# Attention heads taken two at a time on TensorE: scores by row halves into two banks, values by column halves

## The reference, cut to what matters

```python
scores = q[j] @ k[j].T / 8 + bias      # 256 x 256, only the causal three 128x128 blocks
p = softmax(scores)                    # diff heads: p = softmax(s0) - lam * softmax(s1)
out = p @ v[j]                         # 28 products: 8 moba, 4 diff (128 wide), 8 + 8 windowed
```

## Time and profile before

| what | value |
|---|---|
| median of 3 runs | 1296.03 us (1295.26 to 1300.27) |
| the profiled execution's own time | 1300.93 us |
| its span, first to last instruction | 1299.1 us |
| time outside the span | 1.8 us |
| mean granted TensorE clock | 0.988 of full speed |

### The profile page before, as it was taken

How to read it: one execution, slowest core, us unless ns; L and a number is a source line. 1 busy time by engine, 2 the same in 40 slices (tenths; PEclk the granted TensorE clock), 3 DMA queues, 4 the chain that set the end, 5 groups by cost and what they waited for, 6 DMA issues and landing times. The chain is left out here.

```text
span 1299.1 us, 27195 instructions
## 1 busy us (share of the span) xinstructions
PE 1257.0 (97%) x10208; PEld 1217.9 (94%) x10208; DVE 875.5 (67%) x1457; ACT 708.3 (55%) x1221; POOL 403.9 (31%) x376
## 2 busy tenths in 40 slices
PE   8998879799999999999999999999999999999997
PEld 7988779799999999998999999999988999999997
DVE  6656667577777765666667777855766567777755
ACT  4654558445566654555544666644455445666642
POOL 2020100722333421130135643413620237434313
PEclk9999989999999999999999999999999999999999
DMA  7633344466465666554565466666444563666662
GB/s 249 191 114 114 98 130 130 130 194 184 157 190 185 189 184 188 156 160 131 149 191 165 132 193 184 186 188 187 131 146 130 167 191 115 181 192 192 181 185 89
DMA packets 60288, 212.70 MB, mean 164 GB/s; under 512 B 6688, under 2 KB 7968, under 8 KB 60064
## 3 DMA queue, kind: packets, MB, share of 16 engines
q1 hardware_dynamic: 60192, 211.39, 53.4%
HBM read 210.31 MB, written 1.05 MB: 163 GB/s over the span
## 5 line engine op out<-in xcount | busy, mean ns | idle before, releaser
L1337 DVE TENSOR_TENSOR wlo<-raw,whi 128x1024 fp32r<-128x1024 f32 (+1 forms) x400 | 494.8, 1238 | 267.0 <-ACT whi L697 262.6
L1022 PE MATMUL bank<-xhi,whi 128*128 128x256 f32 x2240 | 642.0, 287 | 13.7 <-DVE wlo L1337 12.0
L1023 PE MATMUL bank<-xlo,whi 128*128 128x256 f32 x2240 | 628.5, 281 | 0.0
L1024 PE MATMUL bank<-xhi,wlo 128*128 128x256 f32 x2240 | 628.4, 281 | 0.0
L697 ACT ACTIVATE whi<-raw 128x1024 fp32r<-128x1024 f32 (+1 forms) x400 | 415.5, 1040 | 155.9 <-PE bank L1024 150.8
L1022 PEld LDWEIGHTS bank<-xhi,whi 128*128 128x128 f32 x2240 | 427.0, 191 | 30.6 <-DVE wlo L1337 17.0
L1024 PEld LDWEIGHTS bank<-xhi,wlo 128*128 128x128 f32 x2240 | 424.7, 190 | 0.0
L1023 PEld LDWEIGHTS bank<-xlo,whi 128*128 128x128 f32 x2240 | 423.0, 189 | 0.6
L598 POOL TENSOR_TENSOR fprod<-ugate,uval 128x256 f32<-128x256 f32 x66 | 92.0, 1394 | 213.3 <-DVE uval L1683 207.7
L1022 PE MATMUL bank<-fhi,whi 128*128 128x256 f32 x528 | 148.7, 282 | 0.0
L1024 PE MATMUL bank<-fhi,wlo 128*128 128x256 f32 x528 | 148.4, 281 | 0.0
(11 more groups left out here) (202 smaller groups left out, 1311.6 us busy)
## 6 DMA issues: line engine op xcount, KB each, us to landing
raw<-in_w_win SPq DMA_DIRECT2D x140, 512.0 KB, 3.5
raw<-in_w_up SPq DMA_DIRECT2D x132, 512.0 KB, 3.6
raw<-in_w_down SPq DMA_DIRECT2D x48, 448.0 KB, 3.5
raw<-in_w_merge SPq DMA_DIRECT2D x32, 512.0 KB, 4.0
raw<-in_w_out SPq DMA_DIRECT2D x24, 512.0 KB, 3.5
raw<-in_w_down SPq DMA_DIRECT2D x24, 512.0 KB, 3.5
x<-in_x SPq DMA_DIRECT2D x4, 256.0 KB, 4.9
rgw<-in_rg_w SPq DMA_DIRECT2D x1, 1024.0 KB, 10.6
```

The source lines that it names most:

```text
L1022: pe.matmul(ps, whi[:, slot, w], hi, start=first, stop=False)
L1023: pe.matmul(ps, whi[:, slot, w], lo, start=False, stop=False)
L1024: return pe.matmul(ps, wlo[:, slot, w], hi, start=False, stop=last)
L1337: dve.tensor_tensor(wlo[:, n % RING, w], raw[:, n % RING, w], whi[:, n % RING, w].bitcast(f32), ALU.subtract) \
```

## The change

Scores, values and their waits are regrouped by pairs of heads.

- TensorE "scores" takes two heads: their q and k lie in rows 0 to 63 and 64 to 127. The four matmuls go head A, head B (first 128 queries), head A, head B (the other 128). Head A writes `ps_score`, head B writes `ps_stat`, a bank that was free in these stages.
- TensorE "values" takes two 64-wide heads: A, B (first half of the keys), A, B (second half), head A to columns 0 to 63 and head B to columns 64 to 127 of one bank. Differential heads stay single.
- VectorE, ScalarE and GpSimd do in one "scores" step what they did in two, and read the bank of the head. "weights" stays one head at a time.
- The slots: moba scores in 13, 15, 17, 19, weights in 15 to 22 as before, values in 17, 19, 21, 23. Differential: turns of v one slot earlier (24, 25), scores in 25, 28, 31, 33, weights in 28, 31, 34, 36, values in 29, 32, 35, 37. Second and third layer: scores in 9, 13, 17, 21, weights in 11, 12, 15, 16, 19, 20, 23, 24, values in 13, 17, 21, 25.
- The order within a slot is now values, weights, scores; it was weights, scores, values.

```diff
-    for j in range(MOBA_H):
-        at(b + 13 + j, "scores", j)
-        at(b + 15 + j, "weights", j)
-        at(b + 16 + j, "values", j)
+    for pair in range(MOBA_H // 2):
+        at(b + 13 + 2 * pair, "scores", pair)
+        for i in range(2):
+            at(b + 15 + 2 * pair + i, "weights", 2 * pair + i)
+        at(b + 17 + 2 * pair, "values", 2 * pair)
     for half in range(NQT):
-        at(b + 25 + half, "turn_v", 1, half)
-    for j in range(2 * DIFF_H):
-        at(b + 26 + j, "scores", MOBA_H + j)
-        if j % 2:
-            at(b + 28 + j, "weights", MOBA_H + j // 2)
-            at(b + 29 + j, "values", MOBA_H + j // 2)
+        at(b + 24 + half, "turn_v", 1, half)
+    for h, n in enumerate((25, 28, 31, 33)):
+        at(b + n, "scores", MOBA_H // 2 + h)
+        at(b + n + 3, "weights", MOBA_H + h)
+        at(b + n + 4, "values", MOBA_H + h)
...
-        for j in range(8):
-            g = 16 + 8 * l + j
-            at(b + 9 + 2 * j, "scores", g)
-            at(b + 11 + 2 * j, "weights", MOBA_H + DIFF_H + 8 * l + j)
-            at(b + 12 + 2 * j, "values", MOBA_H + DIFF_H + 8 * l + j)
+        for pair in range(4):
+            w = MOBA_H + DIFF_H + 8 * l + 2 * pair
+            at(b + 9 + 4 * pair, "scores", MOBA_H // 2 + DIFF_H + 4 * l + pair)
+            for i in range(2):
+                at(b + 11 + 4 * pair + i, "weights", w + i)
+            at(b + 13 + 4 * pair, "values", w)
...
-    order = ("rg_split", "rg_scan", "turn_v", "turn_v2", "rope", "weights", "scores", "values")
+    order = ("rg_split", "rg_scan", "turn_v", "turn_v2", "rope", "values", "weights", "scores")
...
+        def score_bank(j):
+
+            return (ps_score, ps_stat)[j % 2]
...
-            def step_scores(j):
-                u, q, k, qp, kp, slope = head(j)
-                if j < 16:
-                    pe.wait_ge(copied, 12 if j < 8 else 24)
+            def step_scores(pair):
+                heads = (2 * pair, 2 * pair + 1)
...
-                wait(pe, logits, j)
-                pe.matmul(ps_score[:, 0:P], u[qp:qp + HD, q, 0:P], u[kp:kp + HD, k, 0:P], start=True, stop=True)
-                pe.matmul(ps_score[:, P:3 * P], u[qp:qp + HD, q, P:2 * P], u[kp:kp + HD, k, :], start=True, stop=True,
-                          skip_group_check=True).then_inc(scored, 1)
+                wait(pe, logits, 2 * pair)
+                for rows, cols, across in ((0, P, P), (P, S, S)):
+                    for j in heads:
+                        u, q, k, qp, kp, slope = head(j)
+                        mm = pe.matmul(score_bank(j)[:, rows:rows + across], u[qp:qp + HD, q, rows:cols], u[kp:kp + HD, k, 0:across],
+                                       start=True, stop=True, skip_group_check=True)
+                        if rows:
+                            mm.then_inc(scored, 1)
...
-                pe.matmul(ps_out[off:off + m, 0:S], v[:, 0, c:c + m], probT[:, w % 2, 0:S], start=True, stop=False)
-                pe.matmul(ps_out[off:off + m, P:S], v[:, 1, c:c + m], probT[:, w % 2, S:3 * P], start=False, stop=True).then_inc(valued, 1)
+                m = P // len(jobs)
+                for half in range(NQT):
+                    for i, job in enumerate(jobs):
+                        c = w * HD + m * i if w < 8 else (w - 8) * P if w < 12 else HD * i
+                        mm = pe.matmul(ps_out[m * i:m * i + m, half * P:S], v[:, half, c:c + m],
+                                       probT[:, job % 2, half * S:half * P + S], start=half == 0, stop=half == 1, skip_group_check=True)
+                        if half:
+                            mm.then_inc(valued, 1)
```

More of the change, by code:

```diff
@@ L530, in _ @@
             pool.memset(ones[:], 1.0).then_inc(ones_set, 1)
-            def step_scores(j):
[L533 to L540, removed]
+            def step_scores(pair):
+                for j in (2 * pair, 2 * pair + 1):
+                    slope = head(j)[5]
+                    if slope is None:
+                        return
+                    if j == 0:
+                        pool.wait_ge(load_const, 16)
+                    wait(pool, logits, j - 1)
+                    pool.tensor_scalar(table[:, j % 2, :], cst("alibi", 3 * P), 2.0 ** -slope, None, ALU.mult).then_inc(tabled, 1)
             def step_pool_sums(l):
@@ L770, in step_turn_v2, with step_scores @@
                 act.activation(u2[:, VT2, :], ps_misc[:, 0:S], ACT.Copy).then_inc(misc_read, 1)
[L772 to L782, removed]
+            def step_scores(pair):
+                for j in (2 * pair, 2 * pair + 1):
+                    act.wait_ge(logits, j + 1)
+                    s = j % 4
+                    for q, (a, b) in enumerate(((0, P), (P, 3 * P))):
+                        e = act.activation(prob[:, s, a:b], prob[:, s, a:b], ACT.Exp, bias=small[:, NEGM + 2 * s + q:NEGM + 2 * s + q + 1],
+                                           accum_out=small[:, ROWSUM + 2 * s + q:ROWSUM + 2 * s + q + 1])
+                    if j >= 16:
+                        sk = (j - 16) % 8
+                        e = act.activation(small[:, SINK + 2 * s:SINK + 2 * s + 2], small[:, NEGM + 2 * s:NEGM + 2 * s + 2], ACT.Exp,
+                                           bias=col(f"sinks{(j - 16) // 8}", sk))
+                    e.then_inc(expd, 1)
             def step_weights(w):
@@ L790, in step_values @@
             def step_values(w):
-                if w < 8 and w % 2 == 0 or w >= 12 and w % 2 == 0:
-                    return
-                act.wait_ge(valued, w + 1)
+                act.wait_ge(valued, w + (1 if 8 <= w < 12 else 2))
                 if w < 8:
@@ L1150, in step_rope, with step_scores @@
                 pe.matmul(ps_misc[:, 0:S], swap, u2[:, tile, :], start=True, stop=True).then_inc(misc_done, 1)
-            def step_scores(j):
-                u, q, k, qp, kp, slope = head(j)
-                if j < 16:
-                    pe.wait_ge(copied, 12 if j < 8 else 24)
-                else:
-                    i = (j - 16) % 8
-                    pe.wait_ge(roped, 5 * ((j - 16) // 8) + 2 + i // 2)
-                wait(pe, logits, j)
-                pe.matmul(ps_score[:, 0:P], u[qp:qp + HD, q, 0:P], u[kp:kp + HD, k, 0:P], start=True, stop=True)
-                pe.matmul(ps_score[:, P:3 * P], u[qp:qp + HD, q, P:2 * P], u[kp:kp + HD, k, :], start=True, stop=True,
-                          skip_group_check=True).then_inc(scored, 1)
+            def step_scores(pair):
+                heads = (2 * pair, 2 * pair + 1)
+                if pair < MOBA_H // 2 + DIFF_H:
+                    pe.wait_ge(copied, 12 if pair < MOBA_H // 2 else 24)
+                else:
+                    i = pair - MOBA_H // 2 - DIFF_H
+                    pe.wait_ge(roped, 5 * (i // 4) + 2 + i % 4)
+                wait(pe, logits, 2 * pair)
[6 more added lines that the diff above has]
+                            mm.then_inc(scored, 1)
             def step_weights(w):
@@ L1173, in step_values @@
             def step_values(w):
[L1174 removed]
+                jobs = (w,) if 8 <= w < 12 else (w, w + 1)
+                pe.wait_ge(turn_read, jobs[-1] + 1)
                 if w < 8:
                     pe.wait_ge(misc_read, MISC[("turn_v", 0, 1)] + 1)
[L1177 removed]
+                    v = va
                 elif w < 12:
                     pe.wait_ge(misc_read, MISC[("turn_v", 1, 1)] + 1)
[L1180 removed]
+                    v = vc
                 else:
[L1182 removed]
                     pe.wait_ge(misc_read, MISC[("turn_v2", (w - 12) // 8)] + 1)
                     v = u2[:, VT2, :].rearrange("p (h n) -> p h n", h=2)
[L1185 removed]
                 wait(pe, out_read, outs_before(w))
[L1187 to L1188 removed]
+                m = P // len(jobs)
[6 more added lines that the diff above has]
+                            mm.then_inc(valued, 1)
             def step_diff_stats():
@@ L1487, in step_prepare_cosines @@
                 dve.memset(small[:, 91:92], 0.0).then_inc(prep, 1)
[L1489 to L1510, removed]
@@ new lines, in step_scores @@
+            def step_scores(pair):
+                for j in (2 * pair, 2 * pair + 1):
+                    s = j % 4
+                    dve.wait_ge(scored, j + 1)
+                    slope = head(j)[5]
+                    if slope is not None:
+                        dve.wait_ge(tabled, j + 1)
+                        tab = table[:, j % 2, :]
+                    else:
+                        tab = cst("slide", 3 * P)
+                    if j >= 4:
+                        dve.wait_ge(turned, weight_job(j - 4) + 1)
+                    neg_max = small[:, NEGM + 2 * s:NEGM + 2 * s + 2]
+                    for q, (a, b) in enumerate(((0, P), (P, 3 * P))):
+                        r = dve.tensor_tensor_reduce(out=prob[:, s, a:b], in0=score_bank(j)[:, a:b], in1=tab[:, a:b], scale=HD ** -0.5,
+                                                     scalar=-3.0e38, op0=ALU.add, op1=ALU.max, accum_out=neg_max[:, q:q + 1])
```

(7 more changed lines are left out.)

## The result

The changed kernel takes 1264.0 us (median of 4 runs, 1262.1 to 1267.4) against 1296.2 us (4 runs, 1295.3 to 1300.3) of the kernel before on the same chip: 0.9752 of its time, 95% interval 0.9712 to 0.9792. The profiled execution takes 1262.84 us, its span is 1261.0 us, its mean granted clock 0.984 of full speed.

A forecast was written before the change was run, and what follows sets the result against it. TensorE, busy 97% of the span, was taken as the bound, with its own work and waits. 9.3 + 10.3 - 3.6 + 6.0 = 22.0 us off 1296.0 gave 1274.0 us, range 1267 to 1287.

The forecast's parts named there:

- part 2: Scores and values pairs outside differential heads: two heads partly overlap in the array, 0.43 a pair, 10.3 us won (0 to 15.4).
- Part 1: TensorE outside the differential heads: 49 fewer changes of matmul shape at 0.19 us each, 9.3 us won.
- rival C: Pairs outside the differential heads overlap in full: 26.5 us won, so 1269.5 us; chance 0.12.
- Part 3: Windowed heads, slots 17 and 21: VectorE's bunched work delays the next weights, four stalls grow by 0.9, 3.6 us lost.
- The four turns named: Turns near slots 19 and 23 of layers two and three, behind gated_conv: stall goes from 0.3 to 1.2 us.
- Rival E: Each of the eight windowed pairs makes TensorE wait, and the differential heads give little: 1283 to 1291 us; chance 0.06.
- Part 4: Differential heads: shorter stalls, fewer shape changes, overlap of four pairs and no old slow stretch, 6.0 us won (3 to 8).
- The first stall: Differential heads: the turn behind unit 28 waits 2.6 us for weights; a second stall of 2.6 follows behind unit 31.
- The 1.5 us of the slow stretch that goes: Differential heads: the slow stretch of the kernel before disappears, 1.5 us won.
- The 1.2 charged for new stretches: Differential heads: one or two new slow stretches may follow the 2.6 us stalls; 1.2 us taken off the gain.
- Rival B: The array's halves don't overlap; only shape changes and the differential heads' ring count: 14.8 us won, so 1281; chance 0.20.
- Rival D: Each step between array halves costs like a shape change, 84 steps: 1297 (no change) or 1304 us (slower); chance 0.12.

The follow-up runs named there:

- experiment 2: Changed kernel with all of head A's matmuls ahead of head B's in each pair, scores and values, instead of alternating: 1265.6 us, 0.9778 of the kernel before.
- Experiment 8: Changed kernel with gated_conv two slots later (19 and 23), behind the weights of both heads of the pair: 1260.4 us, 0.9722 of the kernel before.
- the repeat: The changed kernel measured and profiled once more without an edit, for the scatter: 1262.2 us, ratio 0.974, span 1260.8 us.
- experiment 9: Changed kernel with weights and values of the first three differential heads one slot later: 1259.9 us, 0.9742 of the kernel before.
- Experiment 5: Kernel before with three idle 128x128 turns behind the last values step of each windowed layer, heads unchanged: 1291.5 us, 0.9974.
- experiment 3: Changed kernel with head A's matmuls first and TensorE waiting for A's results before head B's, so nothing of these pairs overlaps: 1280.9 us, 0.9913.
- experiment 10: Changed kernel with gated_conv two slots later, later differential weights and values, idle turns behind layer_norm_shift and ahead of layer 1's feed-forward output: 1254.2 us, 0.9678.

## Why the prediction was right and wrong

The bound, the direction and the size class were right: TensorE's own work sets the time, and what leaves it is won. The forecast of 22.0 us fell 10 short, and the step that failed is part 2.

**Part 1 held**, as far as a sum can show it. With the overlap at its measured size the moba stretch should give 11 x 0.19 + 8 x 0.62 + 0.3 of pace = 7.4; it gave 7.6. No run changes the number of shape changes alone.

**Part 2 is the step that was wrong.** "If starts stay in order and one tile can't take its next record before its last has streamed, only the neighbours A' and B, B' and the next A, overlap." Starts don't stay in order between tiles: a pair's span is one head's, 0.85 against 0.85, and experiment 2 shows it with A wholly ahead of B. The term is 0.62 a pair, not 0.43: 24 pairs outside the differential heads give 4.6 us more, and four within them 0.8. Its upper bound, 0.64, was right, and rival C (0.12) was the mechanism that happened; its 1269.5 still lies 5.5 above the result. The value in the middle was chosen by an argument about issue order that no row bore.

**Part 3 held in its place and not quite in its size.** The four turns named came 1.6 and 1.4 us late in each layer, start to start, where 1.2 was expected; no other turn of the windowed heads came more than 0.4 late. The 0.4 more at slots 19 is part 2's error again: a pair of values and a pair of scores cost TensorE 1.85 and not 2.27, so it is at the turn 0.42 sooner. The kernel before had 0.3 at slots 19 but only 0.14 at slots 23. So 6.1 - 0.9 = 5.2 us were lost instead of 3.6. Experiment 8 takes these stalls away and wins 4.6. Rival E (all eight pairs stall) did not come.

**Part 4 held by its sum and not by its items.** The stretch gave 6.5 by the repeat and 5.4 by the first profile, where 6.0 was said; with full overlap it is 6.8. The first stall came out as 2.9, for 2.6. The second came out as 1.5, for 2.6; where the clock stayed at full speed it was 2.5 (experiment 9), so the low clock in between is what the working lacked. The 1.5 us of the slow stretch that goes are an estimate from the earlier trace rows, where the window has a clock of 0.52 and 17 matmuls in 3.4 us, for the 30 that fit at 0.114. The 1.2 charged for new stretches no run shows; with one of 3.4 us the way from turn to turn grew by some 0.6, with one of 6.8 by 1.8 to 2.0 (experiment 9). In slots 35 and 36, where 0.45 and 0.8 were worked out, the repeat waits 0.7 for ScalarE's copy and 0.5 for the weights, and the first profile does not wait. No scores step waits any more, as said.

**What was not in the sum** is the pace of the units. 4.0 us of the 31.4 come from the two stretches behind the heads, and about 1.7 more from units between the heads (26 slow units there before, 10 in the repeat of after, at 0.107 each). Experiment 5 shows that this is a cause of its own, to be had without the change. It could have been read in the kernel before: by stretch, its matmuls have means of 276 or of 281 ns. The earlier trace rows both stand at 0.114 apart, and so I took one pace for all.

Together: 22.0 + 4.6 + 0.8 - 1.6 + 5.7 of pace = 31.5, measured 31.4 by stretches and 32.2 by medians. That it comes so near is in part luck, since the differential heads alone vary by 1.1 between the two profiles. Both errors that counted, the overlap and the pace, went the same way. Rival B (no overlap) fell by the rows, and experiment 3, which is nearly that kernel, gives 1280.9 where B said 1281, though its fences cost some of that. Rival D fell with the 7 ns between the tiles.

Two things stay open. Why the step ahead sets the pace of the units behind it was not found; nor was why the long feed-forward inputs change from the fast pace to the slow one by themselves, at another unit in each execution (0 to 44 of their 44 units were slow in the profiles). All 44 slow is 4.7 us more than all fast, so this could be most of the scatter of some 3 us between executions of one kernel; that is not shown, since one execution of each run has a trace.

## What to carry to other kernels

Where two small matmuls fit into different row or column halves of the array, put them side by side, in either order: the second was free here (0.85 us for the scores of two heads and of one, 0.80 and 0.79 for their values), and what has to be worked out is the engine that reads the results, whose work now comes in bunches. Before a step is moved on an in-order engine, list what stands between it and the next thing that the bound engine waits for: by the stretches, one slot further was 9.7 us worse and two slots further 4.6 better. And look at the mean length of the main matmul by stretch, not in one place: a difference of 5 ns in 281 was nearly a fifth of this gain.

## What the runs showed of the hardware that was not expected

- Float32 matmuls of two records each, in two row halves or two column halves, run at the same time in full: 0.85 us for the scores of two heads and of one, 0.80 and 0.79 for the values, with starts 7 ns apart when they alternate and 14 ns when all of one head's stand ahead in the program (experiment 2).
- Matmuls of one shape at full granted clock have two lengths, 276 and 281 ns (after in 609 to 659 us, before in 632 to 684), and two paces, 0.1134 and 0.118 us; a pace mostly lasts until another step comes between, and a 128x128 turn there is nearly always followed by the fast one (226 of 238). Three idle turns cost 0.34 us ahead of the feed-forward output of layer 1 in experiment 10, and a unit at the fast pace is 0.107 shorter.
- A stretch at a granted clock of 0.50 shortens the next stall of TensorE, and costs more than it gives: with none of it between two stalls (one trace) the second was 2.5 us and 12.95 us lay from turn to turn; with 3.4 us of it 1.5 and some 13.6 (four traces), with 6.8 us of it 1.5 and 14.7 to 14.9 (two).
